# One block for the attention of the sampled tokens and of the prompt, and one added wait at TensorE

## The chip, the cores and the metric

The kernel runs on one core of one Trainium2 chip. The metric is the time of one execution on the device, in microseconds (us). The kernel before takes 1823.34 us as the median of three runs, from 1818.98 to 1825.59.

## The reference, cut to what matters

One layer of a hybrid decoder is computed for a prompt of 1024 tokens and for 8 sequences of 4 sampled tokens, each with 1024 cached tokens. A projection is followed by attention and an output projection, and then by a feed-forward part.

```python
o_n, o_f, state = mixer_prompt(h, ...)    # 1024 tokens of the prompt
o_n, o_f, state = mixer_sample(h, ...)    # 8 x 4 sampled tokens, paged cache
# attend_block, for both:
#   NSA heads (8): o_c = softmax(q kc + bias) vc        compressed blocks
#                  o_s = softmax(q ks_sel + bias) vs_sel selected blocks
#                  o_w = softmax(q kw + bias) vw        window of 512
#                  o_n = g0*o_c + g1*o_s + g2*o_w
#   FoX heads (8): o_f = softmax(q kf + decay) vf
# finish_layer:   concat(rms_norm(o_n), rms_norm(o_f)) @ w_o, then the SwiGLU feed-forward part
```

## The kernel before, in words

The program is written per engine, with the order of each engine's instructions set by hand, and with semaphores between the engines. It has four stages, each in a `Block` of its own: A (`build_a`, norm and projection), B (`build_b`, attention of the sampled tokens), C (`build_c`, attention of the prompt) and D (`build_d`, output projection and feed-forward part). At the end of a block all engines meet, and no engine begins the next block's instructions before.

**Stage B** works in two rounds of four sequences. The end of a round on TensorE is `turn_probs` of the FoX probabilities (L1209), `fox_values` (L1365, 1367) and `turn_output` (`("ot_fox", r)`, L1356). VectorE copies the values out of PSUM (L1609) and then the turned output into `o_foxT` (L1612), which ScalarE stores to `oT_dram` (`store_fox`, L1006; semaphore `fox_out_last`). Stage B also prepares stage C. SP, whose queue carries nearly all loads, issues in this order: the tables (`load_tables`), `q_nsa` of head pair 0, `k_cmp` and `v_cmp`, the keys and values that all pairs share (`load_shared`: `k_slc`, `k_win`, `v_slc`, `v_win` last), and the FoX part of pair 0 (`load_fox_keys`: four loads into `q_parts`, one into `k_parts`; `load_fox_rest`: two into `decay`, and `v_fox` last). The twelve transfers up to `v_win` raise `kv_loaded` to 192; the eight from `q_parts` to `v_fox` raise `fox_loaded[0]` to 128. VectorE ends with three fills of `bias_cmp` (L1615 to 1617), and GpSimd then expands them into `bias_cx` (L1901, `first_table`).

**Stage C** walks through units (pair of heads, tile of 128 queries, kind, head of the pair) in the order of `UNITS`: first the compressed units `cmp` of pair 0 (u = 0, 1), then for each tile `slc`, `win` and `fox`. Each unit goes: scores on TensorE (`scores`, L2026 for `cmp`, L2044 and 2045 for the others), bias and maximum on VectorE (`peak`, L2254 to 2260 for `cmp`, L2269 for others), exponent on ScalarE (`exponent`, L2126, 2129), turning on TensorE (`turn`, L2053), copies (L2139), and the product with the values (`values`). The first scores wait for `kv_loaded` 192. The order on VectorE at the start is: `peak(0)`, `peak(1)`, then `high_part` (L2326) for `nsa` 0, `fox` 0, `nsa` 1, `fox` 1, and only then `peak(2)`. `high_part("fox", 0)` waits for `fox_loaded[0]` 128. SP begins stage C with waits for the stores of stage B, loads `mixT` (L1994), and then issues the loads of head pair 1 with no further wait; they go to the other half of the buffers.

Of the kernel before, what the change touches and what calls it, by code (L numbers as in the profile page):

```python
# [13 lines left out]
P = 128  # L14
# [88 lines left out]
def program(nc, a, o, c):  # L103
# [4 lines left out]
    with root:  # L108
# [823 lines left out]
def build_b(nc, a, o, c, env):  # L932
# [12 lines left out]
    with ctx:  # L945
# [62 lines left out]
        with nc.Block() as block:  # L1008
            @block.sync
            def _(sp):  # L1010
                page_ids = {}

                def read_pages(s):
                    for p in range(PAGES):
                        page_ids[s, p] = page_of(sp, pages, s, p)

                def load_chunks(c):
                    for b in range(2):
                        read_pages(2 * c + b)
                    PE.wait(sp, ("ct", c - 2, 1, 3))  # L1020
                    for b in range(2):
                        for p in range(PAGES):
                            src = a["cache_nsa_kv"][0, bass.ds(page_ids[2 * c + b, p], 1)].rearrange("o p a g d -> (o p) (a g d)")[:, 0:2 * P]
                            sp.dma_start(chunks[:, c % 2, b, p, :], src).then_inc(chunk_loaded[c % 2], 16)
                    page_ids.clear()

                def fill(f):
                    which, r, p = FILLS[f]
                    if f >= SLOTS:
                        kind, r0, p0 = FILLS[f - SLOTS]  # L1030
                        PE.wait(sp, ("kf", r0, p0, SEQ4 - 1) if kind == "K" else ("use_v", r0, p0))
                    at = 0 if which == "K" else 512
                    for q in range(SEQ4):
                        src = a["cache_fox_kv"][0, bass.ds(page_ids[r * SEQ4 + q, p], 1)].rearrange("o p a h d -> (o p) (a h d)")
                        sp.dma_start(fox_ring[:, f % SLOTS, q, :], src[:, at:at + 512]).then_inc(ring_loaded[f % SLOTS], 16)

                for chunk_tile in (2, 3):
                    load_chunks(chunk_tile)
                PE.wait(sp, ("ct", 2, 1, 3))
                sp.dma_start(chunks[:, 0, 0], nsa_kv_prompt[0, 0].rearrange("(t p) a g d -> p t (a g d)", p=P)[:, :, 0:2 * P]).then_inc(chunk_loaded[0], 16)  # L1040
                for r in range(RN):
                    page_ids.clear()
                    for q in range(SEQ4):
                        read_pages(r * SEQ4 + q)
                    if r == 0:
                        PE.wait(sp, ("ct", 4, 1, 1))
                        for f in range(4):
                            fill(f)
                        PE.wait(sp, ("vc", 8))
                        DVE.wait(sp, ("ev", ("vc", 8)))  # L1050
                    for f in range(r * 2 * PAGES + (4 if r == 0 else 0), (r + 1) * 2 * PAGES):
                        fill(f)
                PE.wait(sp, ("s_fox_new", RN - 1))
                load_tables(sp, env, c)
                load_queries(sp, env, 0, env["kv_loaded"])
                sp.wait_ge(cmp_stored, 32)
                sp.wait_ge(filled, 2)
                for half in range(2):
                    part = slice(half * DH, (half + 1) * DH)
                    sp.dma_start(k_cmp[part, :, 0:NC], kc_dram.rearrange("(g d) n -> d g n", g=G)).then_inc(env["kv_loaded"], 16)  # L1060
                    sp.dma_start(v_cmp[half * DH:half * DH + NC, half, :], vc_dram).then_inc(env["kv_loaded"], 16)
                load_shared(sp, env, nsa_kv_prompt)
                PE.wait(sp, ("use_v", RN - 1, 3))
                load_fox_keys(sp, env, 0, env["fox_loaded"][0])
                load_fox_rest(sp, env, fox_kv_prompt, 0)

            @block.gpsimd
            def _(pool):
                ids = {}

                def read_four(r):
                    ids.clear()
                    for p in range(PAGES):
                        for q in range(SEQ4):
                            ids[p, q] = page_of(pool, pages, r * SEQ4 + q, p)

                def load_nsa(r):
                    if r:
                        PE.wait(pool, ("o_nsa", r - 1))
                    for q in range(SEQ4):  # L1080
                        pool.dma_start(win_rows[:, :, q, :], a["state_win_kv"][0, r * SEQ4 + q].rearrange("(t p) a g d -> p t (a g d)", p=P)).then_inc(win_loaded, 16)
                    for p in range(PAGES):
                        for q in range(SEQ4):
                            pool.dma_start(nsa_page[:, p, q, :], a["cache_nsa_kv"][0, bass.ds(ids[p, q], 1)].rearrange("o p a g d -> (o p) (a g d)")[:, 2 * P:4 * P]).then_inc(nsa_loaded[p // 4], 16)

                pool.memset(chunksT[:, :, :, 4, :], 0.0).then_inc(cleared, 1)
                pool.dma_start(k_new[:, 2:6, :], zT[TILE["fox_kv"]:TILE["fox_kv"] + 4, :, T:N].rearrange("n p t -> p n t")).then_inc(new_loaded, 16)
                pool.wait_ge(pages_loaded, 16)
                read_four(0)
                load_nsa(0)  # L1090
                for r in range(RN):
                    four = slice(r * SEQ4, (r + 1) * SEQ4)
                    pool.dma_start(v_new[:, r, 0:P], nsa_kv_sample[0, four, :, 3].rearrange("s t g d -> (s t) (g d)")).then_inc(v_new_loaded, 16)
                    for q in range(SEQ4):
                        pool.dma_start(v_new[q * TS:(q + 1) * TS, r, P:2 * P],
                                       win_kv_sample[0, r * SEQ4 + q, WIN - TS:WIN, 1].rearrange("t g d -> t (g d)")).then_inc(v_new_loaded, 16)
                    pool.dma_start(v_new[:, r, 2 * P:2 * P + 512], fox_kv_sample[0, four, :, 1].rearrange("s t h d -> (s t) (h d)")).then_inc(v_new_loaded, 16)
                read_four(1)
                DVE.wait(pool, ("ev", ("kc", 1)))
                pool.dma_start(kc_dram, kc[:, 8 * NC:9 * NC]).then_inc(cmp_stored, 16)  # L1100
                DVE.wait(pool, ("ev", ("vc", 8)))
                pool.dma_start(vc_dram, vc[:, 8, :]).then_inc(cmp_stored, 16)
                load_nsa(1)

                for r in range(RN):
                    with nc.allow_non_contiguous_dma(reason="four tokens of four sequences per head"):
                        DVE.wait(pool, ("ev", ("ot_nsa", r)))
                        for g in range(G):
                            for q in range(SEQ4):
                                pool.dma_start(by_head[:, g * R:(g + 1) * R, T + r * 16 + q * TS:T + r * 16 + (q + 1) * TS],  # L1110
                                               o_nsaT[g * DH:(g + 1) * DH, q * 32 + g * R * TS:q * 32 + (g + 1) * R * TS].rearrange("p (h t) -> p h t", t=TS)).then_inc(nsa_out_stored, 16)
                        if r < RN - 1:
                            DVE.wait(pool, ("ev", ("ot_fox", r)))
                            store_fox(pool, r, fox_out_stored)
                pool.wait_ge(filled, 5)
                for e in range(2):
# [2310 lines left out]
```

## Time and profile before

| what | value |
|---|---|
| median of three runs | 1823.34 us |
| the profiled execution | 1820.88 us, of which the span of the trace is 1819.2 us |
| TensorE busy | 1722.9 us (95%) |
| VectorE busy | 1007.6 us (55%) |
| ScalarE busy | 723.6 us (40%) |
| GpSimd busy | 300.9 us (17%) |
| last work of stage B on TensorE, start | 563.63 us |
| first work of stage C on TensorE, start | 573.79 us |
| mean granted clock of TensorE, share of full speed | 0.98 |

Times in rows are counted from the start of the span. PE is the matmul side of TensorE and PEld its loading of weights, DVE is VectorE, ACT ScalarE, POOL GpSimd, and SPq, ACTq and POOLq the queues in which an engine issues its DMAs. `[9.54 <-X]` behind a row says that the engine had been idle for 9.54 us before it, and that X came last. PEclk is the granted clock of TensorE (1.00 is 2.4 GHz, 0.50 is 1.2 GHz). The DMA share is how much of the 16 DMA engines' time was busy. L12 is line 12 of the kernel before.

### The profile page before, as it was taken

The numbers are of one execution on the slowest core, as the hardware profiler recorded it, in microseconds if no ns is written. First come the engines' busy times: TensorE is split into PE (matmuls) and PEld (weight loads), VectorE is DVE, ScalarE is ACT, GpSimd is POOL, SyncE is SP. The second block draws the span as 40 slices with busy tenths as digits, with TensorE's granted clock in tenths as the row PEclk, the third lists the DMA queues.
The fourth block names the chain that finished last, engine by engine and source line by source line (L and its number), as shares of the span: only waits on it lengthen the run. The fifth ranks groups of instructions, "written<-read, shape, count | busy, mean of one in ns | idle before, by whom it ended". The sixth has DMA issues, their size and how long they took to land. (4 is left out here: it accounts for less than half of the span.)

```text
span 1819.2 us, 35393 instructions
## 1 busy us (share of the span) xinstructions
PE 1722.9 (95%) x13557; PEld 1577.7 (87%) x13557; DVE 1007.6 (55%) x1891; ACT 723.6 (40%) x1439; POOL 300.9 (17%) x629
## 2 busy tenths in 40 slices
PE   8999999799895999999998999999999999999998
PEld 7999998676573888888886879999999999999998
DVE  4533332124353666667665567766656664666665
ACT  5111010222231778676775642233333333344343
POOL 3000024410502434453530000000000000000000
PEclk9999999899996999999998999999999999999998
DMA  5548876645999103030202232222222225131112
GB/s 147 183 131 192 227 226 117 205 135 177 299 347 266 63 1 106 1 105 2 94 1 74 90 122 83 72 83 85 80 71 71 82 96 203 65 132 44 47 47 102
DMA packets 145682, 212.63 MB, mean 117 GB/s; under 512 B 23850, under 2 KB 102105, under 8 KB 145459
## 3 DMA queue, kind: packets, MB, share of 16 engines
q1 hardware_dynamic: 113714, 143.36, 24.8%
q0 software_dynamic: 16480, 52.41, 9.5%
q10 hardware_dynamic: 15328, 14.72, 3.3%
q8 instruction: 103, 1.69, 0.4%
q14 instruction: 57, 0.46, 0.1%
HBM read 163.11 MB, written 51.49 MB: 118 GB/s over the span
## 5 line engine op out<-in xcount | busy, mean ns | idle before, releaser
L191 PE MATMUL psum<-h_parts,down_hi 128*128 128x352 f32 x528 | 171.6, 325 | 5.9 <-DVE h_parts L3277 4.3
L191 PE MATMUL psum<-x_hi,w_hi 128*128 128x352 f32 x528 | 170.7, 323 | 1.4 <-issue 1.3
L192 PE MATMUL psum<-h_parts,down_hi 128*128 128x352 f32 x528 | 170.5, 323 | 0.0
L193 PE MATMUL psum<-h_parts,down_lo 128*128 128x352 f32 x528 | 170.4, 323 | 0.0
L192 PE MATMUL psum<-x_lo,w_hi 128*128 128x352 f32 x528 | 170.4, 323 | 0.0
L193 PE MATMUL psum<-x_hi,w_lo 128*128 128x352 f32 x528 | 170.3, 323 | 0.0
L191 PE MATMUL psum<-hf_hi,op_hi 128*128 128x264 f32 x576 | 163.5, 284 | 0.6 <-DVE silu L3258 0.6
L193 PE MATMUL psum<-hf_hi,op_lo 128*128 128x264 f32 x576 | 163.5, 284 | 0.0
L192 PE MATMUL psum<-hf_lo,op_hi 128*128 128x264 f32 x576 | 163.3, 284 | 0.0
L2129 ACT ACTIVATE probs<-psum,neg_max 128x640 f32<-128x640 f32 (+7 forms) x192 | 139.7, 728 | 20.0 <-DVE neg_max L2269 10.6
L2053 PE MATMUL psum<-ident,probs 128*128 128x128 f32 x848 | 129.1, 277 | 5.2 <-ACT probs L2129 4.0
L2139 ACT COPY probsT<-psum 128x512 f32<-128x512 f32 (+3 forms) x240 | 110.8, 484 | 54.6 <-PE psum L2053 53.1
L191 PE MATMUL psum<-t_hi,op_hi 128*128 128x264 f32 x432 | 123.0, 285 | 0.0
L193 PE MATMUL psum<-t_hi,op_lo 128*128 128x264 f32 x432 | 122.6, 284 | 0.0
L192 PE MATMUL psum<-t_lo,op_hi 128*128 128x264 f32 x432 | 122.5, 284 | 0.0
L2053 PEld LDWEIGHTS psum<-ident,probs 128*128 128x128 f32 x848 | 102.2, 141 | 18.7 <-ACT probs L2129 7.9
L734 DVE SCALAR_TENSOR_TENSOR z_stage<-psum,rstd 128x352 f32<-128x352 f32 x66 | 30.4, 516 | 158.2 <-PE psum L193 147.2
L191 PEld LDWEIGHTS psum<-hf_hi,op_hi 128*128 128x128 f32 x576 | 108.3, 188 | 0.8 <-DVE silu L3258 0.8
L193 PEld LDWEIGHTS psum<-hf_hi,op_lo 128*128 128x128 f32 x576 | 108.3, 188 | 0.0
L192 PEld LDWEIGHTS psum<-hf_lo,op_hi 128*128 128x128 f32 x576 | 108.3, 188 | 0.0
L191 PEld LDWEIGHTS psum<-h_parts,down_hi 128*128 128x128 f32 x528 | 99.1, 188 | 8.7 <-DVE h_parts L3277 6.3
L191 PEld LDWEIGHTS psum<-x_hi,w_hi 128*128 128x128 f32 x528 | 99.2, 188 | 2.8 <-issue 2.5
(455 smaller groups left out, 4258.0 us busy)
## 6 DMA issues: line engine op xcount, KB each, us to landing
fox_ring<-in_cache_fox_kv SPq DMA_DIRECT2D x128, 256.0 KB, 5.7
zT<-z_stage SPq DMA_DIRECT2D x22, 528.0 KB, 4.3
w_ring<-in_w_in POOLq DMA_DIRECT2D x22, 512.0 KB, 5.6
down_ring<-in_w_ffn_down SPq DMA_DIRECT2D x44, 256.0 KB, 2.7
raw<-in_w_ffn_gate SPq DMA_DIRECT2D x9, 1024.0 KB, 7.8
raw<-in_w_ffn_up SPq DMA_DIRECT2D x9, 1024.0 KB, 5.3
h_dram<-stage POOLq DMA_DIRECT2D x8, 1056.0 KB, 6.0
nsa_page<-in_cache_nsa_kv POOLq DMA_DIRECT2D x64, 128.0 KB, 6.2
```

The costliest lines, as they stand in the source:

```text
L191: nc.tensor.matmul(dst, w_hi, x_hi, start=start, stop=False, skip_group_check=onto)
L192: nc.tensor.matmul(dst, w_hi, x_lo, start=False, stop=False, skip_group_check=onto)
L193: return nc.tensor.matmul(dst, w_lo, x_hi, start=False, stop=stop, skip_group_check=onto)
L734: last = nc.vector.scalar_tensor_tensor(out=z_stage[:, s, tok], in0=bank[3 * s + b][:, 0:NB], scalar=scale, in1=rstd[:, tok], op0=ALU.mult ...
L2053: last = nc.tensor.transpose(place(("turn", g))[:, j * P:(j + 1) * P], probs[:, u % 4, (at + j) * P:(at + j + 1) * P], ident[:, :])
L2129: nc.scalar.activation(probs[:, u % 4, 0:n], slot_of(u), ACT.Exp, bias=neg_max[:, u % 4:u % 4 + 1], scale=-1.0 if turned_over(u) else 1.0, ...
L2139: nc.scalar.copy(dst, place(("turn", g))[:, 0:n * P]).then_inc(copied["A"], 1)
```

## The change

The blocks of stages B and C become one: the block is opened before `build_b`, both stages write their instructions into it, and it is closed after `build_c`. The meeting between stages A and B and that between C and D stay. TensorE gets one wait as the last thing of stage B: for VectorE's copy of `("ot_fox", RN - 1)`, since stage C's scores use the PSUM banks that stage B used. All else is the same text, one level of indentation less.

```diff
@@ program
         env = dict(locals())
         build_a(nc, a, o, c, env)
+        middle = root.enter_context(ExitStack())
+        env["block"] = middle.enter_context(nc.Block())
         build_b(nc, a, o, c, env)
...
                 build_c(nc, a, o, c, env, mixT, low, w_o, w_o_loaded, squares)
+                middle.close()
                 build_d(nc, a, o, env, mixT, w_o, w_o_loaded, squares, hf_hi, hf_lo, tiles, x1, ffn_out)
@@ build_b
-        with nc.Block() as block:
-            @block.sync
+        block = env["block"]
+        @block.sync
...
@@ build_b, tensor
             for r in range(RN):
                 keys(r)
                 DVE.wait(pe, ("gate_fox", r))
                 for k in range(3):
                     turn_probs(("pt_fox", r, k), {"fox": s_fox})
                 fox_values(r)
                 turn_output(r)
+            wait_ev(("ot_fox", RN - 1))
@@ build_c
-        with nc.Block() as block:
-            @block.sync
+        block = env["block"]
+        @block.sync
...
```

## Rows read from the trace of the kernel before

**Rows 1.** The page: its first line, and the busy time of all engines.
```profile
span 1819.2 us, 35393 instructions
PE 1722.9 (95%) x13557; PEld 1577.7 (87%) x13557; DVE 1007.6 (55%) x1891; ACT 723.6 (40%) x1439; POOL 300.9 (17%) x629
```

**Rows 2.** Windows of 50 us: PE, PEld, DVE, ACT, POOL busy, clock, DMA, GB/s.
```profile
550.00:600.00 50.00, 32.63 (x219) 21.13 (x220) 17.12 (x51) 13.15 (x38) 9.38 (x28) 0.70 1.02 276
```

**Rows 3.** Timeline of all engines, end of stage B to start of C.
```profile
564.29 0.48 DVE L1612 COPY so_foxT<-psum 128x32 f32<-128x32 f32 x4 [0.81 <-PE psum L1356]
...
564.81 1.29 ACTq L1006 DMA_DIRECT2D oT_dram<-so_foxT  x2
...
565.80 2.87 POOL L1901 COPY bias_cx<-bias_cmp 128x64 f32<-128x64 f32 x16 [15.47 <-DVE bias_cmp L1617]
...
573.79 3.68 PE L2026 MATMUL psum<-k_cmp,q_nsa 64*128 64x64 f32 x32 [9.54 <-PEq L1008]
575.86 0.70 DVE L2254 TENSOR_TENSOR psum<-psum,bias_cx 128x512 f32<-128x512 f32 x1 [10.12 <-PE psum L2026]
...
580.39 0.28 DVE L2326 CAST high_nsa<-q_nsa 128x256 fp32r<-128x256 f32 x1
...
584.13 0.30 DVE L2326 CAST high_fox<-q_parts 128x256 fp32r<-128x256 f32 x1 [3.45 <-DMA v_fox<-out]
...
585.30 0.28 DVE L2269 CUSTOM_DVE_ANT_0 psum<-psum,bias 128x128 f32<-128x128 f32 x1
...
585.67 0.37 ACT L2129 ACTIVATE probs<-psum,neg_max 128x128 f32<-128x128 f32 x1 [1.80 <-DVE neg_max L2269]
...
586.19 0.48 PE L2053 MATMUL psum<-ident,probs 128*128 128x128 f32 x1 [1.42 <-ACT probs L2129]
```

**Rows 4.** Timeline of SP's queue: last loads of stage B, first of C.
```profile
555.88 6.69 SPq L1829 DMA_DIRECT2D v_win<-vw_nat  x1
...
569.68 0.46 SPq L1848 DMA_DIRECT2D v_fox<-out  x1
573.68 4.03 SPq L1994 DMA_DIRECT2D mixT<-oT_dram  x1
577.76 6.28 SPq L1820 DMA_DIRECT2D q_nsa<-zT  x4
```

**Rows 5.** The tile `v_fox`, its two loads from 535 to 600 us.
```profile
DMA to landing us min/median/max: 12.6/13.5/14.4
```

**Rows 6.** DMA issues, 540 to 600 us: size of one, median us to landing.
```profile
mixT<-oT_dram SPq DMA_DIRECT2D x1, 128.0 KB, 11.7
...
oT_dram<-so_foxT ACTq DMA_DIRECT2D x2, 16.0 KB, 6.1
```

**Rows 7.** Windows: columns as in rows 2, the end of B and the start of C.
```profile
570.00:582.00 12.00, 3.96 (x34) 3.83 (x34) 4.61 (x9) 1.19 (x2) 0.72 (x1) 0.50 0.99 280
...
576.00:579.00 3.00, 1.47 (x14) 1.28 (x13) 2.86 (x6) 0.60 (x1) 0.00 (x0) 0.50 1.02 392
...
582.00:585.00 3.00, 2.77 (x14) 2.58 (x13) 0.87 (x3) 0.58 (x1) 0.50 (x1) 0.50 0.83 188
585.00:588.00 3.00, 1.77 (x6) 1.49 (x7) 2.86 (x12) 1.45 (x6) 2.47 (x5) 0.50 1.04 231
588.00:591.00 3.00, 3.00 (x9) 1.73 (x8) 1.83 (x7) 1.67 (x7) 0.39 (x1) 0.61 1.05 231
591.00:594.00 3.00, 2.69 (x25) 2.20 (x24) 2.33 (x7) 2.55 (x7) 1.21 (x3) 1.00 1.00 274
...
600.00:603.00 3.00, 3.00 (x29) 2.54 (x28) 2.87 (x9) 2.36 (x5) 0.19 (x1) 1.00 0.03 8
```

**Rows 8.** Timeline: the meeting between A and B, then between C and D.
```profile
322.69 0.52 SPq L360 DMA_DIRECT2D out<-nat  x1
...
326.93 5.64 PE L1148 MATMUL psum<-ident,chunks 128*128 128x128 f32 x32 [5.18 <-PEq L255]
...
957.96 0.45 POOL L2230 TENSOR_TENSOR squares<-squares,o_square 128x128 f32<-128x128 f32 x1
...
958.75 1.04 ACT L2947 CAST d_m_hi<-mixT 128x1024 fp32r<-128x1024 f32 x1 [0.91 <-PEq L1988]
```

More of the change, by code:

```diff
@@ new lines, in keys @@
+                job = ("s_cmp", r)
+                dst = bank_of(job)
+                wait_ev(("kc", 1))
+                for q in range(SEQ4):
+                    s = r * SEQ4 + q
+                    last = nc.tensor.matmul(dst[rows_of(q), 0:NC], q_nsa[:, s, :], kc[:, s * NC:(s + 1) * NC], start=True, stop=True)
+                PE.done(last, job)
+                pe.wait_ge(win_loaded, 64 * (r + 1))
+                turn_four(("kw", r, 0), lambda q: win_rows[:, 0, q, 0:P])
+                bank = bank_of(("s_win", r))
@@ new lines, in keys @@
+                for n in range(1, 4):
+                    turn_slc(n)
+                    nsa_scores("use_s", r, n - 1, bank)
+                job = ("pt_imp", r)
+                dst = bank_of(job)
+                DVE.wait(pe, ("norm_cmp", r))
+                apart(pe)
+                PE.done(nc.tensor.transpose(dst[0:NC, 0:P], p_imp[:, :], ident[:, :]), job)
+                nsa_scores("use_s", r, 3, bank)
+                pe.wait_ge(nsa_loaded[1], 256 * (r + 1))
+                turn_slc(4)
@@ new lines, in keys @@
+                turn_slc(5)
+                bank = bank_of(("s_slc", r, 1))
+                nsa_scores("use_s", r, 4, bank)
+                job = ("imp", r)
+                dst = bank_of(job)
+                wait_ev(("pt_imp", r))
+                apart(pe)
+                PE.done(nc.tensor.matmul(dst[:, 0:16], impT[:, :], overlap[:, :], start=True, stop=True), job)
+                turn_slc(6)
+                nsa_scores("use_s", r, 5, bank)
+                turn_slc(7)
+                nsa_scores("use_s", r, 6, bank)
@@ new lines, in keys @@
+                nsa_scores("use_s", r, 7, bank)
+                new_scores(("s_slc_new", r), r, 0)
+                job = ("imp_sum", r)
+                dst = bank_of(job)
+                wait_ev(("imp", r))
+                PE.done(nc.tensor.matmul(dst[:, 0:16], group_sum[:, :], imp_rows[:, :], start=True, stop=True), job)
+                DVE.wait(pe, ("scan", r))
+                turn_fox(r, 0)
+                bank = fox_decay(r, 0)
+                for n in range(1, 4):
+                    turn_fox(r, n)
+                    fox_scores(r, n - 1, bank)
@@ new lines, in keys @@
+                DVE.wait(pe, ("gate_win", r))
+                for k in range(2):
+                    turn_probs(("pt_w", r, k), {"cmp": s_cmp, "win": s_win})
+                fox_scores(r, 3, bank)
+                turn_fox(r, 4)
+                DVE.wait(pe, ("gate_slc", r))
+                for k in range(3):
+                    turn_probs(("pt_slc", r, k), {"slc": s_slc})
+                bank = fox_decay(r, 1)
+                turn_fox(r, 5)
+                fox_scores(r, 4, bank)
+                nsa_values(r)
@@ new lines, in keys @@
+                turn_fox(r, 6)
+                fox_scores(r, 5, bank)
+                turn_fox(r, 7)
+                fox_scores(r, 6, bank)
+                job = ("ot_nsa", r)
+                dst = bank_of(job)
+                wait_ev(("o_nsa", r))
+                PE.done(nc.tensor.transpose(dst[:, 0:P], o_nsa[:, :], ident[:, :]), job)
+                fox_scores(r, 7, bank)
+                job = ("s_fox_new", r)
+                dst = bank_of(job)
+                for q in range(SEQ4):
+                    s = r * SEQ4 + q
+                    for p in range(4):
+                        nc.tensor.matmul(dst[rows_of(q), 0:NEW], q_fox[:, s, 32 * p:32 * p + 32], k_new[:, 2 + p, r * NEW:(r + 1) * NEW],
+                                         start=(p == 0), stop=(p == 3), skip_group_check=True)
@@ new lines, in keys, with turn_output @@
+                for q in range(SEQ4):
+                    last = nc.tensor.matmul(dst[rows_of(q), q * TS:(q + 1) * TS], neg_pick[:, q, :], ck[:, PAST:L], start=False, stop=True, skip_group_check=True)
+                PE.done(last, job)
+            def turn_output(r):
+                job = ("ot_fox", r)
+                dst = bank_of(job)
+                wait_ev(("o_fox", r))
+                for p in range(4):
+                    last = nc.tensor.transpose(dst[:, p * P:(p + 1) * P], o_fox[:, p * P:(p + 1) * P], ident[:, :])
+                PE.done(last, job)
@@ new lines, in fox_values @@
+            def fox_values(r):
+                wait_ev(("pt_fox", r, 2))
+                bank = bank_of(("o_fox", r))
+                for n in range(8):
+                    slot = ring_wait(pe, "V", r, n)
+                    for q in range(SEQ4):
+                        last = nc.tensor.matmul(bank[rows_of(q), :], ptT[:, PT["fox"] + n, rows_of(q)], fox_ring[:, slot, q, :], start=(n == 0), stop=False)
+                    PE.done(last, ("use_v", r, n))
+                last = nc.tensor.matmul(bank, ptT[0:NEW, PT["fox"] + 8, :], v_new[:, r, 2 * P:2 * P + 512], start=False, stop=True)
+                PE.done(last, ("use_v", r, 8))
@@ new lines, in _, with evict_ct @@
+            compress(0)
+            compress(1)
+            pe.wait_ge(setup_loaded, 16 * SETUP_LOADS)
+            pe.wait_ge(new_loaded, 16 * NEW_LOADS)
+            for r in range(RN):
+                keys(r)
+                DVE.wait(pe, ("gate_fox", r))
+                for k in range(3):
+                    turn_probs(("pt_fox", r, k), {"fox": s_fox})
+                fox_values(r)
+                turn_output(r)
+            wait_ev(("ot_fox", RN - 1))
+        def evict_ct(eng, copy, steps, job):
+            _, t, kv, half = job
+            st, first, _ = CT_TILES[t]
+            PE.wait(eng, job)
+            if st:
+                PE.wait(eng, ("hid", 0, 1, 1))
+            steps.done(copy(chunksT[:, kv, :, first + half // 2, half % 2 * 32:half % 2 * 32 + 32].rearrange("p j c -> p c j"),
+                            psum[:, B.bank[job], :].rearrange("p (c j) -> p c j", j=CS)), ("ev", job))
@@ new lines, in evict_keys @@
+        def evict_keys(eng, copy, steps, job):
+            kind, r, n = job[:3]
+            PE.wait(eng, job)
+            if kind == "kf":
+                slot = (n * SEQ4 + job[3]) % 12
+                if n >= 3:
+                    PE.wait(eng, ("use_f", r, n - 3))
+                elif r:
+                    PE.wait(eng, ("use_f", r - 1, 7))
+                dst = kT_fox[:, slot, :]
+            elif kind == "kw":
+                if n == 3:
+                    PE.wait(eng, ("use_w", r, 0))
+                elif r:
+                    PE.wait(eng, ("use_s", r - 1, 7))
+                dst = kT_nsa[:, n % 3, :]
+            else:
+                PE.wait(eng, ("use_s", r, n - 3) if n >= 3 else ("use_w", r, n + 1))
+                dst = kT_nsa[:, (n + 1) % 3, :]
+            steps.done(copy(dst, psum[:, B.bank[job], :]), ("ev", job))
@@ new lines, in _, with scores, turn, values @@
+        @block.tensor
+        def _(pe):
+            pe.wait_ge(filled, 2)
+            def scores(u):
+                hp, m, kind, e = UNITS[u]
+                g = hp // 2
+                lo, n = key_tiles(m, kind)
+                slot = slots[:, 512 * SLOT_BANK[u]:]
+                if kind == "cmp":
+                    if e == 0:
+                        if hp == 0:
+                            pe.wait_ge(kv_loaded, 192)
+                        else:
+                            pe.wait_ge(q_loaded[hp % 2], 64 * ((hp + 1) // 2))
+                    for j in range(4):
+                        for par in range(2):
+                            i = QT - 1 - 2 * j - par
+                            part = slice(par * DH, (par + 1) * DH)
+                            last = nc.tensor.matmul(slot[:, 256 + par * 256 + j * DH:256 + par * 256 + (j + 1) * DH],
+                                                    q_nsa[part, (hp + 1) % 2, e, i * P:(i + 1) * P].bitcast(F32), k_cmp[part, g, :], start=True, stop=True)
+                    last.then_inc(scored, 1)
+                    return
+                if kind == "fox":
+                    if m == 0 and e == 0:
+                        pe.wait_ge(fox_loaded[hp % 2], fox_loads(hp))
+                    k = k_fox[:, hp % 2, e, :]
+                else:
+                    k = (k_slc if kind == "slc" else k_win)[:, g, :]
+                of = "fox" if kind == "fox" else "nsa"
+                q_low, q_high = query_of(hp * QT + m, of)
+                if e == 0:
+                    POOL.wait(pe, ("low", of, hp * QT + m))
+                dst = slot_of(u)
+                w = n * P // 2 if n > 4 else n * P
+                for at in range(0, n * P, w):
+                    keys = k[:, lo * P + at:lo * P + at + w]
+                    nc.tensor.matmul(dst[:, at:at + w], q_high[:, e, :], keys, start=True, stop=False)
+                    last = nc.tensor.matmul(dst[:, at:at + w], q_low[:, e, :], keys, start=False, stop=True)
+                last.then_inc(scored, 1)
+            def turn(u):
+                for g in entries_of(u):
+                    _, at, n = ENTRIES[g]
+                    wait_place(pe, ("turn", g))
+                    for j in range(n):
+                        last = nc.tensor.transpose(place(("turn", g))[:, j * P:(j + 1) * P], probs[:, u % 4, (at + j) * P:(at + j + 1) * P], ident[:, :])
+                    last.then_inc(turned, 1)
+            def values(p):
+                hp, m, kind, _ = UNITS[2 * p]
+                if kind == "cmp":
+                    return
+                final = entries_of(2 * p + 1)[-1]
+                for engine in "AV":
+                    pe.wait_ge(copied[engine], copied_through(final, engine))
+                g, macro = hp // 2, hp * QT + m
+                if kind == "slc":
+                    if macro:
+                        CLOSE_ACT.wait(pe, ("out", macro - 1))
+                    if m == 0:
+                        first = entries_of(unit_no(hp, -1, "cmp", 1))[-1]
+                        for engine in "AV":
+                            pe.wait_ge(copied[engine], copied_through(first, engine))
+                    _, _, blk, half = cmp_place(m)
+                    for e in range(2):
+                        nc.tensor.matmul(outs[e * DH:(e + 1) * DH, 0:P], v_cmp[:, half, g * DH:(g + 1) * DH],
+                                         cmpT[:, hp % 2, e, blk * P:(blk + 1) * P], start=True, stop=True)
+                lo, n = key_tiles(m, kind)
+                col = (KINDS.index(kind) + 1) * P
+                for t in range(n):
+                    for e in range(2):
+                        v = v_fox[:, hp % 2, lo + t, e, :] if kind == "fox" else (v_slc if kind == "slc" else v_win)[:, lo + t, g, :]
+                        last = nc.tensor.matmul(outs[e * DH:(e + 1) * DH, col:col + P], v, probsT[:, (2 * p + e) % 4, t * P:(t + 1) * P],
+                                                start=(t == 0), stop=(t == n - 1))
+                last.then_inc(summed, 1)
+            def natural(macro):
+                CLOSE_ACT.wait(pe, ("out", macro))
+                wait_place(pe, ("natural", macro))
+                for k in range(4):
+                    last = nc.tensor.transpose(place(("natural", macro))[:, k * P:(k + 1) * P], outT[:, k, :], ident[:, :])
+                CLOSE_PE.done(last, ("natural", macro))
+            def mix(macro):
+                POOL.wait(pe, ("sum", macro, 1))
+                wait_place(pe, ("mix", macro))
+                dst = place(("mix", macro))
+                nc.tensor.transpose(dst[:, 0:P], o_sum[:, macro % 2, :], ident[:, :])
+                CLOSE_PE.done(nc.tensor.transpose(dst[:, P:2 * P], weighed[:, macro % 2, 3, :], ident[:, :]), ("mix", macro))
+            for p in ROUNDS:
+                for e in range(2):
+                    for u in pair_of(p + 1)[e:e + 1]:
+                        if SLOT_BEFORE[u] is not None:
+                            pe.wait_ge(exp_done, SLOT_BEFORE[u] + 1)
+                        scores(u)
+                    for u in pair_of(p)[e:e + 1]:
+                        pe.wait_ge(exp_done, u + 1)
+                        turn(u)
+                if p - 2 in ENDS:
+                    natural(ENDS[p - 2])
+                if p - 3 in ENDS:
+                    mix(ENDS[p - 3])
+                if 0 <= p - 1 < NP:
+                    values(p - 1)
```

1543 lines of the change are left out of this document (656 added, 887 removed).

## The prediction

> **What bounds the kernel now.** I read the page first, then the span in windows, then the boundary between stages B and C engine by engine. TensorE is busy for 1722.9 of 1819.2 us [rows 1], so over the whole kernel 96 us of idle time on TensorE are left to win. The windows show where a good part of it lies: from 550 to 600 us TensorE is busy for only 32.63 of 50 us, at a mean clock of 0.70, while the DMA engines are full (share 1.02, 276 GB/s) [rows 2]. That is the stretch which the change touches. A low busy share of TensorE beside a full DMA share asks the reader to look at what the engines wait for, not only at how long they stand still.
>
> The timeline of all engines tells that [rows 3]. VectorE's last copy of stage B begins at 564.29 and takes 0.48 us. TensorE then stands for 9.54 us, until 573.79, and what came last is named as its own sequencer at L1008, the line of stage B's block. The queue of SP shows who came last to the meeting [rows 4]: SP issued `v_fox` from 569.68 to 570.14, and the next thing it issued, `mixT`, began at 573.68. So the meeting holds everything for 573.68 - 570.14 = 3.5 us past the last issue. That is what the change removes.
>
> But the same timeline has a second gate behind the first. TensorE scores the two compressed units from 573.79, VectorE works on them from 575.86, and the cast for `high_nsa` at 580.39 ends that chain at 580.67. Then VectorE is idle for 3.45 us until 584.13, and the releaser is the DMA `v_fox<-out` [rows 3]. That DMA was issued before the meeting, and its landing took 14.4 us, the larger of the two values in the row (569.68 + 14.4 = 584.1) [rows 4, 5]. It is the last of the eight transfers that `high_part("fox", 0)` needs. Everything of stage C past the compressed units hangs on it: VectorE's `peak(2)` follows at 585.30, ScalarE's exponent at 585.67 (released by VectorE), and TensorE's turning at 586.19 (released by that exponent) [rows 3].
>
> **The meeting removed.** First its own size. The meeting between A and B costs 326.93 - (322.69 + 0.52) = 3.7 us after SP's last issue; that between C and D only 958.75 - (957.96 + 0.45) = 0.3 us, where no transfer has just been issued [rows 8]. The one between B and C has 3.5 us and follows an issue, as that of A and B does. So what is taken away is between 0.3 and 3.7 us for an engine that waits for nothing else, and I take 3.5.
>
> Now what each engine waits for without it. TensorE needs `kv_loaded` at 192, whose last transfer is `v_win`. Its landing has no row. It lies between the end of its issue, 555.88 + 6.69 = 562.6, and 573.79, when TensorE used it [rows 3, 4]. Between it and the landing of `v_fox` the queue has four loads of 64 x 1024 values (0.26 MB each), `k_parts` with 1.05 MB, two `decay` rows written 128 times (0.52 MB each) and `v_fox` with 0.52 MB, by the shapes of the tiles: 3.7 MB. At the 280 GB/s of the stretch from 570 to 582 [rows 7] these take 13.1 us, so `v_win` has landed at about 584.1 - 13.1 = 571.0. I take that value, since the rate is read from the very stretch. TensorE can then begin 573.8 - 571.0 = 2.8 us earlier. The table on GpSimd is no hindrance, as it is done at 565.80 + 2.87 = 568.7 [rows 3]. With 562.6 in place of 571.0 the start would be bound by the end of VectorE's copy at 564.8, so it would be 9.0 us earlier; with 573.8, none.
>
> The chain from TensorE's start to the end of the cast takes 580.67 - 573.79 = 6.9 us, at the same clock of 0.50 (TensorE stands for over 6 us either way). It ends at 571.0 + 6.9 = 577.9 in place of 580.7. The next instruction on VectorE still waits for 584.13. So its idle time grows from 3.45 to 6.2 us, and the gain at `peak(2)` is 0. This holds for the whole range of 0 to 9.0 us above: the cover is the landing of `v_fox`, and an earlier chain only makes the wait before it longer. TensorE's scores of units 2 to 4 and ScalarE's copy move earlier too, and also end up waiting for VectorE.
>
> **Does the landing move?** The transfers of pair 0 are all issued before 570.14, so no engine's freedom brings them forward. The DMA engines are at a share of 0.99 from 570 to 582 [rows 7]: the 3.5 us in which SP issued nothing left the transfers with work in their queues. So I take 0 for it. From above it could be 3.5 us, if SP's pause itself had slowed them. From below, it could move back: SP now waits only for the store of `o_foxT` (issued from 564.81 to 566.10, median 6.1 us to land, so until about 572 [rows 3, 6]), and issues `mixT` and the loads of pair 1 some 1 to 2 us sooner. These stand behind `v_fox` in the same queue.
>
> On this order a rule of the Trainium skill bears, "DMA: Bandwidth & Descriptors", the paragraph on HWDGE ordering: descriptors are taken in ring order on each DMA engine, but a later one may complete before an earlier one. The trace has the two landings in order, `v_fox` at 584.1 and `mixT` at 573.68 + 11.7 = 585.4 [rows 4 to 6]. By the first half of the rule the sum stays 0, and the second half speaks for the rival on the slow side below.
>
> **What moved with SP.** The loads of pair 1 (four `q_nsa`, four `q_parts`, `k_parts`, two `decay`, `v_fox`) end about 1 to 2 us earlier. The DMA share is 0.03 at 600 us [rows 7], and pair 1 is computed long after, so this is worth 0. SP's waits for stage B's stores come before them as before.
>
> **The wait added at TensorE.** It waits for the copy that ends at 564.77, and TensorE's transposes before it released that copy at 564.29 [rows 3]: 0.5 us. Behind it on TensorE is all of stage C, and first the wait for `kv_loaded` until about 571.0, which hides it. Were that cover gone it would cost 0.5 us of the 9.0 us that would then be won, and nothing against before, where TensorE stood until 573.79.
>
> **The clock.** TensorE's clock is 0.50 up to 588 us, 0.61 in the three microseconds to 591 and 1.00 after [rows 7]. TensorE had run the compressed scores for 3.68 us on end from 573.79, and the clock was still 0.50 in 576 to 579; it rose only after the dense work that begins at 586.19 [rows 3, 7]. That work does not move. I take 0.
>
> **The sum.** 0 (meeting, behind the landing) + 0 (SP) + 0 (added wait) + 0 (clock) = 0. The profiled execution took 1820.88 us, 1.7 us above its span, and would take 1820.9 us. It was 2.5 us faster than the median of 1823.34, so on the median's scale the forecast is 1823.3 us.
>
> **The rivals.** *The meeting's 3.5 us come through to the end.* For it: TensorE has the low clock and a hole of 9.54 us, and a landing put down as the last releaser is inferred. If SP's pause delays the transfers, removing it brings `v_fox` to 580.6, and VectorE is ready at 577.9. Against it: the DMA engines did not run dry. It would give 1823.3 - 3.5 = 1819.8 us.
>
> *Pair 1 crowds the last load of pair 0.* This is the one on the slow side. Its place is the DMA engines from 577 to 584 us, where `mixT` and the `q_nsa` of pair 1 now arrive sooner, beside `v_fox`. The share there has room for them (0.83 in 582 to 585 [rows 7]), which means that some DMA engines reach the later transfers before others are done with `v_fox`. Price: if both got in front entirely, 0.13 MB + 1.05 MB at 231 GB/s [rows 7] are 5.1 us; if they share evenly, 2.6 us. It decides from the first microsecond by which `v_fox` lands after 584.13, since nothing on VectorE covers it. It would give 1825.9 us, and 1828.4 at most. Against it: the landings came in order, and the loads come only 1 to 2 us sooner.
>
> *The clock rises at another time.* TensorE now works a little from 571.0 and then has a longer hole before 586.19. From 586.19 to 590 it runs at half speed, so a rise right at the start would save at most half of 4 us, 2 us, and a rise put off by as long costs 2 us: 1821.3 or 1825.3 us. The Trainium skill's "TensorE: Matmul & The Clock Gate", Part 1, lets recent activity release the throttle; more activity ahead would then help and a longer hole would not. By it the sum is 0 again, as no denser stretch arises before 586.19.
>
> *The block is one in name only*, and engines still meet: 1823.3 us, the same as the forecast.
>
> **How the numbers follow.** Chances: the forecast (with the last rival, which gives the same) 0.72, the 3.5 us come through wholly or in part 0.14, crowding 0.09, clock 0.05. A measurement can tell about 0.5% from no change, and that is 9.1 us here. None of the cases reaches it: the largest gain is 3.5 us and the largest loss 5.1 us. What is left is what the rows do not show, such as the fetch of instructions where two streams become one, or the spread of the runs (6.6 us from lowest to highest). I give 0.04 to faster, 0.03 to slower, and 0.93 to within 0.5%. The range goes from the first rival less half of the spread, 1819.8 - 3.3 = 1816.5, to the worst of the second, 1828.4.
>
> **What would show it.** In the profile after: TensorE's first L2026 work begins at about 571 (between 565 and 573.8) and its releaser is a DMA, not its sequencer; VectorE's cast for `high_nsa` ends near 578; the next cast still starts at about 584.1, with an idle time of about 6 us before it, released by `v_fox`; the turning at about 586.2 and the clock's rise near 590 stay where they are; `mixT` is issued near 572. The prediction is wrong if that second cast starts over 1 us away from 584.1, measured against the end of stage B, or if the time differs by more than 0.5% though it does not.

## The result, and the profile after

The changed kernel takes 1828.1 us as the median of 17 runs (1825.24 to 1831.72), the kernel before 1823.34 us (1818.98 to 1827.72, also 17). The ratio is 1.0029, with a 95% interval from 1.002 to 1.0037: slower by 0.3%. That is small, but the whole interval lies above 1. Ratios and intervals are taken from all runs, so a ratio need not be the quotient of the two medians. The forecast was no change.

The page of the changed kernel, its first line and the busy time of all engines, shows no more work than [rows 1]: TensorE has the same 13557 matmuls and 3.5 us more of busy time, and the span is 6.1 us longer.

```profile
span 1825.3 us, 35383 instructions
PE 1726.4 (95%) x13557; PEld 1581.0 (87%) x13557; DVE 1008.2 (55%) x1891; ACT 724.4 (40%) x1439; POOL 300.9 (16%) x629
```

The timeline at the place of the change, to be laid beside [rows 3] and [rows 4]. In this execution stage B ends 2.35 us later than in the one before (566.64 against 564.29), so starts are best counted from that copy.

```profile
566.64 0.48 DVE L1616 COPY so_foxT<-psum 128x32 f32<-128x32 f32 x4 [0.81 <-PE psum L1359]
...
571.05 0.43 SPq L1852 DMA_DIRECT2D v_fox<-out  x1
...
572.93 3.68 PE L2030 MATMUL psum<-k_cmp,q_nsa 64*128 64x64 f32 x32 [6.33 <-DMA v_win<-vw_nat]
...
575.08 3.05 SPq L1998 DMA_DIRECT2D mixT<-oT_dram  x1
...
579.53 0.28 DVE L2330 CAST high_nsa<-q_nsa 128x256 fp32r<-128x256 f32 x1
...
584.08 0.29 DVE L2330 CAST high_fox<-q_parts 128x256 fp32r<-128x256 f32 x1 [4.26 <-DMA v_fox<-out]
```

Here the change does what it says. TensorE begins stage C 6.29 us after the copy in place of 9.50 us, and what releases it is the landing of `v_win`, no longer its own sequencer. VectorE then waits for `v_fox` all the same, for 4.26 us.

The loss stands elsewhere, where no line was changed. This is the timeline at the meeting between stages C and D, to be laid beside the last two of [rows 8].

```profile
958.48 0.45 POOL L2234 TENSOR_TENSOR squares<-squares,o_square 128x128 f32<-128x128 f32 x1
963.87 0.33 SPq L2718 DMA_DIRECT2D d_x<-in_x_prompt  x1
963.88 1.04 ACT L2951 CAST d_m_hi<-mixT 128x1024 fp32r<-128x1024 f32 x1 [5.53 <-PEq L187]
```

From the end of GpSimd's last work to ScalarE's first in stage D there are 963.88 - 958.93 = 4.95 us. Before it was 958.75 - 958.41 = 0.34. The growth of 4.61 us is nearly the 4.8 us between the medians. If it is taken off, the interval of the ratio (3.6 to 6.7 us) leaves between 1.0 us less and 2.1 us more for all the rest. The rest of the 6.1 us between the two profiled executions is the 2.35 us by which stage B ended later, 0.97 us in stage D, and 1.83 us less within stage C. The 2.35 us are put down to spread, not to the change: e3_one_dma_in_c below has stages A and B as before and also ends B late, at 566.63.

### The profile page after: what moved, and what is told of

Same layout as the page of the kernel before. It is cut to its first block and busy times, and to the rows that moved or that the text cites. A ratio compares the mean times of both kernels' runs of the same rounds, so it can differ in the third digit from the quotient of the medians.

```text
span 1825.3 us, 35383 instructions
## 1 busy us (share of the span) xinstructions
PE 1726.4 (95%) x13557; PEld 1581.0 (87%) x13557; DVE 1008.2 (55%) x1891; ACT 724.4 (40%) x1439; POOL 300.9 (16%) x629
```

## The experiments

**Theory G.** At the end of a block GpSimd first runs a drain, an instruction that settles something left over from the DMAs that it has issued, and all others wait for it at the meeting. Before, that was paid between B and C, beside transfers that held stage C anyway; merging moved it to the end of C, where nothing covers it. **Rival F:** the branch to the end of the merged block stalls on the fetch of instructions. **Rival S:** the loss arises inside the stages.

In the timelines, *the meeting* is from the end of GpSimd's last `squares` to the start of ScalarE's `d_m_hi`.

**e1_no_pool_drain: the merged block closed without GpSimd's drain.**

```diff
-        env["block"] = middle.enter_context(nc.Block())
+        env["block"] = middle.enter_context(nc.Block(no_gpsimd_drain=True))
@@ end of stage C, GpSimd
+            POOL.wait(pool, ("total", MACROS - 1))
```

> The changed kernel, with the merged block closed without GpSimd's drain (the option no_gpsimd_drain) and a wait of GpSimd on its own last step in its place. Theory G (the meeting after a block in which GpSimd has issued DMAs costs about 5 us from GpSimd's arrival, since GpSimd drains what belongs to its DMAs; merging moved this from a place hidden under the landing of v_fox to the C/D boundary): the gap between GpSimd's last work of C and ScalarE's first of D falls from 4.9 us to at most 0.6, and the time from 1828.1 to about 1823.5 us. Rival F (the branch to the end of the merged block stalls on the fetch of instructions): the gap stays at 4.9 us and the time at 1828. Rival S (the loss comes from within stages B and C): gap and time do not fall together.

Measured: 1821.26 us, 0.9992 of the kernel before (0.9974 to 1.001). The meeting is 956.59 - 956.16 = 0.43 us, and both fell together, as theory G and not rival S expects.

```profile
955.71 0.45 POOL L2234 TENSOR_TENSOR squares<-squares,o_square 128x128 f32<-128x128 f32 x1
...
956.59 1.05 ACT L2952 CAST d_m_hi<-mixT 128x1024 fp32r<-128x1024 f32 x1 [1.01 <-PEq L187]
```

**e2_drain_early: the changed kernel, with GpSimd drained where it stands idle.**

```diff
@@ stage B, GpSimd, after the stores
+            pool.drain()
             pool.wait_ge(filled, 5)
```

> The changed kernel with one drain of GpSimd added after its last store of stage B, where it stands idle for some 15 us. Theory G: the drain is paid there, hidden, and the meeting between C and D costs at most 0.6 us; time about 1823.5 us. Rival F: no difference, 1828 us. If the drain's price hangs on the block having used GpSimd DMAs at all, whatever was drained before: also 1828 us.

Measured: 1822.6 us, ratio 0.9994 (0.9974 to 1.0014), and the meeting is 958.38 - 958.03 = 0.35 us.

```profile
957.58 0.45 POOL L2235 TENSOR_TENSOR squares<-squares,o_square 128x128 f32<-128x128 f32 x1
958.36 0.33 SPq L2719 DMA_DIRECT2D d_x<-in_x_prompt  x1
958.38 1.04 ACT L2952 CAST d_m_hi<-mixT 128x1024 fp32r<-128x1024 f32 x1 [0.93 <-PEq L187]
```

The block, its branch and its closing meeting are those of the changed kernel here, and the price is gone. That rules out F. On F the Trainium skill, "Runtime: NRT & Kernel Launch", section "Instruction fetch mechanics", says that a taken branch out of the fetched pages has to wait for its target; here the engines leave the merged block at the same place as in the changed kernel, and the way out costs no more than 0.35 us in all. Whether the target lay within the fetched pages, no run shows.

**e3_one_dma_in_c and e4_thirty_dmas_in_c: the cause alone, put into the kernel before.**

```diff
@@ stage C, GpSimd (e3: once at the start; e4: after each tile but the last two)
+                pool.dma_start(spare_dram, causal[:, 0:32]).then_inc(spare_stored, 16)
```

> The kernel before with one small GpSimd DMA (128 x 32 values to an unused place) at the start of stage C, and nothing else. Theory G with a fixed price: the meeting between C and D costs about 4.9 us in place of 0.34, time about 1828 us. Theory G with a price per DMA since the last drain (some 105 of them cost 4.6 us): 0.4 us, time about 1823.4. Rivals F and S: meeting and time as before, 1823.3 us.

> The kernel before with 30 small GpSimd DMAs in stage C, one after each tile but the last two. Theory G, fixed price: meeting of 4.9 us as with one DMA. Theory G, price per DMA: 0.34 + 30/105 of 4.6 = 1.7 us. Rivals F and S: 0.34 us. The time is about 1823.3 plus the meeting's growth, and up to 1 us more if issuing the DMAs delays GpSimd's work.

Measured: the meeting is 959.08 - 958.66 = 0.42 us with one and 961.43 - 958.64 = 2.79 us with thirty; the times are 1822.34 us (0.9993, 0.9974 to 1.0013) and 1824.54 us (1.0003, 0.9983 to 1.0024). The timelines at the meeting, first of e3, then of e4:

```profile
958.21 0.45 POOL L2233 TENSOR_TENSOR squares<-squares,o_square 128x128 f32<-128x128 f32 x1
959.07 0.33 SPq L2718 DMA_DIRECT2D d_x<-in_x_prompt  x1
959.08 1.05 ACT L2951 CAST d_m_hi<-mixT 128x1024 fp32r<-128x1024 f32 x1 [1.00 <-PEq L1990]
```

```profile
958.19 0.45 POOL L2232 TENSOR_TENSOR squares<-squares,o_square 128x128 f32<-128x128 f32 x1
961.42 0.33 SPq L2718 DMA_DIRECT2D d_x<-in_x_prompt  x1
961.43 1.05 ACT L2951 CAST d_m_hi<-mixT 128x1024 fp32r<-128x1024 f32 x1 [3.37 <-PEq L1990]
```

In all these runs GpSimd also waits, before it ends stage C, until its added DMAs have landed, so what the meeting pays is not a landing. A fixed price is out: it is 0.08 us for one DMA and 2.45 / 30 = 0.082 us for each of thirty. The two times cannot carry this by themselves, as both intervals include 1. The expectation for e4 by a price per DMA, 1.7 us, was too low, as it had spread stage B's 4.6 us over 105 DMAs.

**e10_sixty_dmas and e11_hundred_five_dmas: more of the same.**

> The kernel before with 60 small GpSimd DMAs in stage C (two after each tile but the last two). One DMA added 0.08 us to the meeting between C and D and thirty added 2.45, so 0.08 each: sixty should add 4.9 us, a meeting of 5.2 us. If the count is capped, it stops near the 4.6 us that stage B's 105 add.

> The same with 105 DMAs, the number that stage B issues. Price per DMA without a cap: a meeting of 0.34 + 8.6 = 8.9 us. With a cap, where stage B's 105 add 4.6 us: 4.9 us, and about the same as with sixty.

Measured, one run each: the meeting is 969.15 - 963.91 = 5.24 us with sixty and 967.25 - 958.33 = 8.92 us with 105; the times are 1832.09 and 1829.94 us. Single times of one kernel differ by several microseconds, so the meetings are what is read here. The timeline of e11 at the meeting:

```profile
957.88 0.45 POOL L2232 TENSOR_TENSOR squares<-squares,o_square 128x128 f32<-128x128 f32 x1
967.23 0.33 SPq L2719 DMA_DIRECT2D d_x<-in_x_prompt  x1
967.25 1.04 ACT L2952 CAST d_m_hi<-mixT 128x1024 fp32r<-128x1024 f32 x1 [9.49 <-PEq L1990]
```

The price of these small stores goes with their number, 0.082 us each from 1 to 105, and there is no cap.

**e12_drain_midway: which of stage B's 105 still count.**

```diff
@@ stage B, GpSimd
             pool.dma_start(vc_dram, vc[:, 8, :]).then_inc(cmp_stored, 16)
+            pool.drain()
             load_nsa(1)
```

> The changed kernel with GpSimd's drain added in the middle of stage B, right after the store of v_cmp: 51 of stage B's 105 DMAs are issued before it and 54 after. In the changed kernel the 105 add 4.61 us to the meeting between C and D, which at the 0.082 us per DMA of the runs with 1, 30, 60 and 105 small DMAs is the price of 56 only. If each of the 105 costs the same 0.044 us, the meeting is now 0.34 + 54 x 0.044 = 2.7 us. If the price is 0.082 us and only the latest 56 or so are still to be paid (the earlier ones were settled on the way), it is 0.34 + 54 x 0.082 = 4.8 us, hardly less than the 4.95 of the changed kernel.

Measured, one run: 1822.14 us beside 1824.06 for the kernel before, and a meeting of 959.21 - 954.45 = 4.76 us.

```profile
954.00 0.45 POOL L2235 TENSOR_TENSOR squares<-squares,o_square 128x128 f32<-128x128 f32 x1
959.19 0.33 SPq L2719 DMA_DIRECT2D d_x<-in_x_prompt  x1
959.21 1.04 ACT L2952 CAST d_m_hi<-mixT 128x1024 fp32r<-128x1024 f32 x1 [5.33 <-PEq L187]
```

So the first 51 weigh nearly nothing, 4.95 - 4.76 = 0.19 us together, and the other 54 add 4.42 us, which is 0.082 us each if all cost the same. That the earlier ones are settled on the way is one reading. An untested rival is that the price hangs on the kind of DMA. The first lot has 49 loads and two stores, the second 36 loads and 18 stores. If only stores counted, the first two would cost 0.1 us each, but the 18 would cost 4.42 / 18 = 0.25 us each, three times as much as the small stores of e3 to e11, although 16 of the 18 move as many packets each as those: GpSimd's queue counts 256 for eight of them and 3360 for the 105 of e11, 32 each. No run has loads alone. The single time of this run, below that of the kernel before, says nothing against a meeting of 4.76 us: single times of one kernel differ by more.

**e8_short_meeting_before: the kernel before, with no drain at the end of stage B alone.**

```diff
@@ build_b
-        with nc.Block() as block:
+        with nc.Block(no_gpsimd_drain=True) as block:
```

> The kernel before with no_gpsimd_drain on stage B's block alone. The meeting between B and C was paced by GpSimd: 5.0 us from its last copy in four traces, whatever SP did. Theory G: stage C now starts when SP arrives or when v_win has landed, near 570 to 571 in place of 573.8; the cast after v_fox stays at about 584, and the time at 1823.3 us. In addition the drain's bookkeeping may be left to the meeting between C and D, which then costs 4.9 us (time 1828) if it counts all DMAs since the last drain, or 0.34 us if it counts the block's. Rival (SP's issues pace the meeting): start unchanged at 573.8.

Measured: 1826.96 us, ratio 1.0021 (1.0008 to 1.0034). The profiled execution took 1846.27 us, with some 20 us more ahead of stage C, so only differences within it are read.

```profile
584.75 0.49 DVE L1612 COPY so_foxT<-psum 128x32 f32<-128x32 f32 x4 [0.81 <-PE psum L1356]
...
592.81 3.68 PE L2026 MATMUL psum<-k_cmp,q_nsa 64*128 64x64 f32 x32 [8.10 <-DMA v_win<-vw_nat]
...
978.13 0.45 POOL L2230 TENSOR_TENSOR squares<-squares,o_square 128x128 f32<-128x128 f32 x1
...
983.53 1.04 ACT L2947 CAST d_m_hi<-mixT 128x1024 fp32r<-128x1024 f32 x1 [5.52 <-PEq L1988]
```

Stage C starts on the landing of `v_win`, so what had held it in the kernel before was GpSimd's drain. And the meeting between C and D, now in a kernel that merges nothing, costs 983.53 - 978.58 = 4.95 us, the same as in the changed kernel. The time is 0.21% longer, 1.5 to 6.2 us by the interval, in which the 4.61 us lie. This is the loss without the change: a drain left out here was paid at the next one.

**e9_only_the_wait: the added wait alone.**

```diff
                     turn_output(r)
+                wait_ev(("ot_fox", RN - 1))
```

> The kernel before with only the wait added at TensorE at the end of stage B. All theories: 0 us, 1823.3 us, since TensorE stands there in any case.

Measured: 1821.87 us, ratio 0.9992 (0.9965 to 1.0018). The wait costs nothing that can be measured, though the interval alone would hide up to 3 us. Its trace also shows how much the cover varies, in VectorE's wait for `v_fox`:

```profile
563.31 0.48 DVE L1613 COPY so_foxT<-psum 128x32 f32<-128x32 f32 x4 [0.81 <-PE psum L1356]
...
579.41 0.28 DVE L2327 CAST high_nsa<-q_nsa 128x256 fp32r<-128x256 f32 x1
...
580.63 0.29 DVE L2327 CAST high_fox<-q_parts 128x256 fp32r<-128x256 f32 x1 [0.94 <-DMA v_fox<-out]
```

**e5_split_before, e7_split_fox_before and e6_split_merged: the cover taken away.** Each reader waits for what it reads. e6 is e2, with its early drain, and this split; its core (e5 is the same on the kernel before, e7 its FoX part alone):

```diff
-            load_queries(sp, env, 0, env["kv_loaded"])
+            load_queries(sp, env, 0, env["first_loaded"])
...
-            load_fox_keys(sp, env, 0, env["fox_loaded"][0])
+            load_fox_keys(sp, env, 0, env["fox_keys"][0])
@@ compressed scores, TensorE
-                            pe.wait_ge(kv_loaded, 192)
+                            pe.wait_ge(env["first_loaded"], 128)
@@ cast of q_parts, VectorE (also the FoX scores, TensorE)
-                    dve.wait_ge(fox_loaded[hp % 2], fox_loads(hp))
+                    dve.wait_ge(env["fox_keys"][hp % 2], 80 * (hp // 2 + 1))
@@ values, TensorE
+                if kind == "fox" and m == 0:
+                    pe.wait_ge(fox_loaded[hp % 2], fox_loads(hp))
```

> The kernel before, with the loads of stage C's start on semaphores of their own, so that each reader waits for what it reads: the compressed scores for q_nsa, k_cmp and v_cmp, the others for k_slc and k_win, the cast of q_parts for q_parts and k_parts, the FoX values for v_fox. The meeting stays. If the landing of v_fox was the cover (my theory), the cast that waited until 584.1 now follows the compressed units at once, at 580.7, and what follows is 3.4 us earlier: 1823.3 - 3.4 = 1819.9 us. The start of stage C stays at 573.8, held by the meeting. Rival: the queues are limited otherwise, nothing moves, 1823.3 us.

> The kernel before with only the FoX loads split (q_parts and k_parts apart from decay and v_fox). With the meeting in place the compressed units end at 580.7 in any case, so this alone should bring the 3.4 us of e5: 1819.9 us. If it brings less than e5, the wait for v_win also counts before the meeting's end.

> The merged kernel with the early drain of GpSimd (as in e2) and the same split of the loads as e5. My theory: stage C starts near 565 to 567 us, the compressed units are done near 574, the cast of q_parts waits for k_parts until about 578, and what follows is about 6 us earlier than in the kernel before: 1817.5 us, which beats both, and 2 to 3 us less than e5. So the worth of merging shows only once its cover is gone. Rival: merging is worth nothing even then, equal to e5.

Measured: e5 1822.85 us (1.0009, 0.9987 to 1.003), e7 1821.08 us (0.9981, 0.9961 to 1.0001), e6 1816.87 us (0.9967, 0.9953 to 0.9982). The timeline of e6:

```profile
565.97 0.48 DVE L1619 COPY so_foxT<-psum 128x32 f32<-128x32 f32 x4 [0.81 <-PE psum L1362]
...
566.83 2.73 PE L2033 MATMUL psum<-k_cmp,q_nsa 64*128 64x64 f32 x32 [0.90 <-DVE so_foxT L1619]
...
573.61 0.28 DVE L2339 CAST high_nsa<-q_nsa 128x256 fp32r<-128x256 f32 x1
...
579.35 0.29 DVE L2339 CAST high_fox<-q_parts 128x256 fp32r<-128x256 f32 x1 [5.46 <-DMA k_parts<-key_parts]
```

TensorE begins stage C 0.86 us after the copy, released by the very wait that the change added. The cast of `q_parts` comes 13.38 us after the copy, where it came after 17.44 in the changed kernel and after 19.84 in [rows 3]. In e5 it comes after 582.62 - 566.33 = 16.29 us and in e7 after 16.33, with no wait for a DMA before it. The expected 1819.9 us, 3.4 us less, was missed by e5, whose interval goes from 2.4 us less to 5.5 us more; e7, with 7.1 us less to 0.2 us more, leaves it open. My 3.4 us were the cover of one execution. In the other traces with the meeting in place it is 1.67 us (e3), 2.55 (e4), 0.94 (e9), 1.18 (e11) and 4.30 (e10), so the gain to expect there is 1 to 4 us. e6 beats both kernels, by 6 us over the kernel before, and its expected 1817.5 us was met. Its median is 6.0 us below that of e5 and 4.2 us below that of e7, and nine of its twelve runs are faster than all of e7's, so its rival, no worth in merging even then, is out.

## Why the prediction was wrong

**The step that failed** is "The meeting removed". It read the 3.5 us between SP's last issue and SP's next as the price of a meeting that "follows an issue", and took [rows 8] for support: 3.7 us after an issue, 0.3 us where there was none. The late one was GpSimd. In [rows 3] its last copy ends at 568.67, and SP and TensorE resume at 573.68 and 573.79. This distance is 5.0 us in the profiled execution, and again in those of e3 (571.02 to 576.02) and e4 (569.51 to 574.51), and so it is in e5, e7, e9 and e11. SP's last issue ends 3.5, 3.3 and 3.1 us ahead of the resumption in the first three, and 2.6, 5.1, 4.4 and 4.3 us in the others. A fixed distance from one engine and a varying one from another names the engine that is waited for. e10 is the exception that fits: there SP ended its last issue only at 577.12, later than GpSimd's 571.95 + 5.0, and went on at 577.61, after 0.5 us. The 3.7 us between A and B were a third thing: SP spent 3.0 of them at the end of its stage A, waiting until its own stores had landed, and GpSimd had issued its last DMA over 30 us earlier (294.80).

```profile
SPq L373 <- DMA out<-nat: 3.0, 1, 3.0
```

Stage C's block was cheap at its end not because no transfer had just been issued, but because GpSimd issues none in it. With the right reading, the meeting that stays could not be left at 0.3 us: the merged block ends with stage B's DMAs still to be drained. That term, 4.6 us, was missing from the sum, and no rival had it. The measured 1828.1 us lies within the range, up to 1828.4, only by luck: that end came from crowding, which did not happen. The prediction also held that less than 0.5% could not be told from no change, where the 17 runs gave an interval from 0.20 to 0.37%.

**What held.** The rest of the sum is 0 as far as can be told. With the drain out of the way (e1, e2), merging alone gives 0.9992 and 0.9994, but their intervals reach from 4.7 us less to 2.6 us more. The changed kernel itself, less the 4.61 us of its meeting, is narrower: from 1.0 us less to 2.1 us more. TensorE's start, released by `v_win`, comes 6.29 us after stage B's copy in the changed kernel, 5.96 in e1 and 6.81 in e2, against 9.50 before: 2.7 to 3.5 us earlier, where 2.8 was forecast. The added wait is 0 as far as e9 can tell. `mixT` is issued 8.44 us after the copy, where about 572, 7.7 us after it, was forecast.

**The cover was right in kind and not in size.** VectorE's wait for `v_fox` was taken as 3.45 us from one execution. Counted from the copy, the cast came at 19.84 us there, and without merging at 18.06 in e3, 18.95 in e4, 19.42 in e8, 17.32 in e9, 22.00 in e10 and 17.56 in e11; with it at 17.44, 17.51, 17.96 and 17.19 in the changed kernel, e1, e2 and e12. The compressed units end after about 16.4 us with the meeting. So by the prediction's own test, that the second cast stay within 1 us when counted from stage B's end, its reading of that landing fails: 19.84 became 17.44. But e9 has 17.32 with nothing merged. Counted from the start of its own issue, `v_fox` lets the cast begin after 12.4 to 13.3 us in all ten other executions, merged or not, and after 14.45 us only in the one that the prediction read. So this is a spread of the issue and the landing, and no effect of the change that can be seen.

**The rivals.** Crowding by pair 1 is not seen: the landing is no later in any merged kernel. That the 3.5 us come through is excluded by the changed kernel's remainder, which is at most 1.0 us of gain. Of the clock, the windows after have it at 0.50 until 591 and at 0.73 in the next three microseconds, where [rows 7] have 0.61 and 1.00:

```profile
588.00:591.00 3.00, 3.00 (x8) 1.91 (x8) 1.77 (x6) 1.73 (x7) 0.44 (x1) 0.50 1.04 231
591.00:594.00 3.00, 3.00 (x22) 2.15 (x21) 1.93 (x5) 2.15 (x6) 1.17 (x3) 0.73 1.01 270
```

If the clock steps once within a slice, it rose at 590.3 before and at 592.6 after, so the sign that it stay near 590 failed. The turning begins at 586.19 before and 586.14 after, behind a hole of 1.42 us [rows 3] and of 2.23 us, and the first product with `v_fox` comes 10.18 us and 10.60 us later:

```profile
586.14 0.48 PE L2057 MATMUL psum<-ident,probs 128*128 128x128 f32 x1 [2.23 <-ACT probs L2133]
...
596.74 1.97 PE L2084 MATMUL psum<-probsT,v_fox 128*64 128x128 f32 x32
```

Before, that product begins at 596.37. So the third rival happened in this pair of executions, for 0.4 us where it had 2. From the second cast to that product it is also 12.66 to 12.67 us in e1 and e2, but 11.77 in e12, and 11.80 to 12.48 in the executions without merging. Whether the change puts the rise off is therefore open. It is too little to explain the loss.

## What to carry to other kernels

In this kernel a meeting cost what the engine that came last still owed: GpSimd's drain between B and C, SP's stores between A and B. Before two blocks are merged, look at each engine's distance from its last work to the resumption, and ask where the debt of the removed meeting is paid then: here GpSimd's drain moved from a covered place to a bare one. A drain of GpSimd put into one of its idle stretches took the debt off the path (e2). And if removing a wait brings nothing because a landing stands behind it, split that landing's semaphore so that each reader waits for its own data. Only with both the early drain and the split did merging pay here (e6).

## What the runs showed that I had not expected

GpSimd's drain costs 0.082 us for each small store that it has issued since the last drain, although all have landed: 0.08, 2.45, 4.90 and 8.58 us over the bare 0.34 for 1, 30, 60 and 105. In the changed kernel it paid 4.61 us for DMAs that it had issued over 400 us earlier (the last until 552.76). Stage B's 105 loads and stores cost as much as 56 of the small stores, and draining after the first 51 takes off 0.19 us only. Either part of them is settled on the way, or the price differs with the kind of DMA. No run here tells which.
